# Attention in a streaming encoder: four steps of one head group moved into the last query tiles, and a third half output tile behind the last values

## The reference

```python
def sink_attention(q, k, v, valid, sinks):
    s = jnp.einsum('bqngd,bknd->bngqk', q, k).astype(jnp.float32)
    s = jnp.where(valid, s, -jnp.inf)
    m = jnp.maximum(jnp.max(s, -1, keepdims=True), sk)      # sk: one learned sink per head
    e = jnp.exp(s - m)
    p = e / (jnp.sum(e, -1, keepdims=True) + jnp.exp(sk - m))
    return jnp.einsum('bngqk,bknd->bqngd', p.astype(v.dtype), v)
# per chunk of 64 queries: its own 64 keys and the 128 before it; 16 heads, 2 key/value heads
q = (h @ w_q); o = attention per chunk; y = o @ w_o
```

## Time and profile before

| | |
|---|---|
| median of the runs | 1477.04 us |
| the profiled execution | 1475.43 us, span 1473.7 us |
| TensorE in the chain that ended last | 97% |
| mean granted TensorE clock | 0.989 |
| query tiles 4 to 7 and the steps, to the full output tiles | 839.03 to 950.37 us |

### The profile page before, as it was taken

One profiled execution on the slowest core, in us unless ns is written; L12 is line 12 of the kernel. 1 busy time (PEld: TensorE's weight loads), 2 busy tenths in 40 slices (PEclk: granted clock), 3 DMA queues, 4 the chain that ended last, 5 costly groups with the idle time before them and its releaser, 6 DMA issues.

```text
span 1473.7 us, 25782 instructions
## 1 busy us (share of the span) xinstructions
PE 1452.4 (99%) x10189; PEld 1411.0 (96%) x10189; DVE 935.5 (63%) x1493; ACT 556.9 (38%) x927; POOL 211.9 (14%) x228
## 2 busy tenths in 40 slices
PE   8999999999999999999999999999999999999998
PEld 7999998999999999999999976899999999999998
DVE  4368776558666667666675647248666766666656
ACT  5155454434233233332335149235323333233225
POOL 1013220221000000000003125121000000000002
PEclk9999999999999999999999989999999999999999
DMA  6422333432221211222203310123121122221102
GB/s 228 143 66 78 119 98 112 151 109 86 86 85 57 85 62 52 85 85 85 85 1 98 112 62 2 42 86 113 60 85 60 54 85 85 85 85 57 57 1 83
DMA packets 100918, 120.63 MB, mean 82 GB/s; under 512 B 8658, under 2 KB 92952, under 8 KB 100584
## 3 DMA queue, kind: packets, MB, share of 16 engines
q1 hardware_dynamic: 100748, 119.73, 24.9%
q10 hardware_dynamic: 108, 0.03, 0.0%
HBM read 108.38 MB, written 11.95 MB: 82 GB/s over the span
## 4 chain that ended last, share of the span: by engine, by line
PE 97%; POOL 1%; DVE 1%; ACT 1%; issue 0%; DMA 0%; ACTq 0%; POOLq 0%; DVEq 0%
PE ps L380 55%; PE ps L540 19%; PE ps L1917 8%; PE ps L391 3%; PE ps L566 2%; PE ps L1001 1%; POOL sum_sq L499 1%; PE ps L1962 1%; PE ps L1975 1%; PE ps L2005 1%; PE ps L1076 1%; PE ps L1594 1%; PE ps L1034 1%; PE ps L1069 0%; PE ps L2001 0%; PE ps L1349 0%
## 5 line engine op out<-in xcount | busy, mean ns | idle before, releaser
L380 PE MATMUL ps<-x_hi,w_hi 128*128 128x320 f32 x1840 | 420.1, 309 | 0.5 <-DVE seq_keys_cols L1241 0.5
L380 PE MATMUL ps<-x_lo,w_hi 128*128 128x320 f32 x1840 | 419.3, 309 | 0.0
L380 PE MATMUL ps<-x_hi,w_lo 128*128 128x320 f32 x1840 | 419.2, 309 | 0.0
L380 PEld LDWEIGHTS ps<-x_hi,w_hi 128*128 128x128 f32 x1840 | 307.4, 188 | 1.3 <-issue 0.7
L380 PEld LDWEIGHTS ps<-x_hi,w_lo 128*128 128x128 f32 x1840 | 307.7, 188 | 0.0
L380 PEld LDWEIGHTS ps<-x_lo,w_hi 128*128 128x128 f32 x1840 | 307.5, 188 | 0.0
L360 ACT ACTIVATE w_hi<-w_raw 128x1024 fp32r<-128x1024 f32 x138 | 145.1, 1060 | 406.4 <-PE ps L380 370.4
L504 DVE TENSOR_TENSOR x_res<-x_res,ps 128x640 f32<-128x640 f32 x192 | 153.8, 818 | 108.2 <-PE ps L380 47.2
L367 DVE TENSOR_TENSOR w_lo<-w_raw,w_hi 128x1024 fp32r<-128x1024 f32 x138 | 170.8, 1244 | 30.8 <-ACT w_hi L360 23.6
L835 POOL TENSOR_TENSOR tail_cols<-up_rows,ones 128x4 f32 (+1 forms) x44 | 50.1, 1139 | 794.9 <-DVE up_rows L628 794.9
L626 DVE TENSOR_TENSOR up_rows<-ps,rstd_cols 128x320 f32<-128x320 f32 x88 | 43.1, 490 | 164.5 <-PE ps L380 164.5
(11 more groups left out here) (283 smaller groups left out, 1901.6 us busy)
## 6 DMA issues: line engine op xcount, KB each, us to landing
w_raw<-in_ffn_w_up_dram SPq DMA_DIRECT2D x44, 1024.0 KB, 5.2
d_raw<-in_ffn_w_down_dram SPq DMA_DIRECT2D x22, 1024.0 KB, 4.9
w_raw<-in_gla_w_in_dram SPq DMA_DIRECT2D x12, 1024.0 KB, 6.1
seq_states<-in_state_gla_dram SPq DMA_DIRECT2D x4, 1024.0 KB, 5.2
out_dram<-seq_states SPq DMA_DIRECT2D x4, 1024.0 KB, 8.6
w_raw<-in_gla_w_out_dram SPq DMA_DIRECT2D x4, 1024.0 KB, 5.7
w_raw<-in_att_w_q_dram SPq DMA_DIRECT2D x4, 1024.0 KB, 6.4
w_raw<-in_att_w_o_dram SPq DMA_DIRECT2D x4, 1024.0 KB, 5.1
```

Source lines behind the costliest of these rows:

```text
L380: mm = pe.matmul(PS[:, 2 * (u0 % 4) + f, 0:HALF], w[:, n0 % 4, k, :], x[:, k, f * HALF:(f + 1) * HALF], start=(k == 0 and a == 0), stop=(k ...
```

## The change

It does four things. `ATT_STEPS` now lists chunks 0 to 3 of group 0, then chunks 0 to 3 of group 1, then the rest as before. On TensorE, scores(1) and scores(2) follow query tile 6; tile 7 is made in two halves with transposes(0) and scores(3) between them; from n = 4 on the loop is as before. VectorE, ScalarE and GpSimd get their parts of steps 0 to 3 ahead of the last query tile's. And a third half output tile stands behind the last values, so that three second halves follow.

```diff
-        ATT_STEPS = [(0, 0), (1, 0), (0, 1), (1, 1)] + [(c, g) for c in range(2, SEQ // CH) for g in range(KVH)]
+        ATT_STEPS = [(c, g) for g in range(KVH) for c in range(4)] + [(c, g) for c in range(4, SEQ // CH) for g in range(KVH)]
...
+            for j in range(KT - 2):
+                gather(j)
+            normalise(0)
+            gather(KT - 2)
+            for n in range(1, 4):
+                normalise(n)
+            gather(KT - 1)
+            for n in range(4, NATT):
+                normalise(n)
...
-                if n == 2:
+                if n == 4:
                     pe.wait_ge(free, u_q(7) + 1)
...
-            for j in range(4, 8):
+            for j in range(4, 7):
                 fm_tile(pe, T_AQ + j, u_q(j))
-                if j in (5, 6):
-                    scores(j - 5)
+                if j == 5:
+                    scores(0)
+            scores(1)
+            scores(2)
+            pe.wait_ge(lo_done, T_AQ + KT)
+            pe.wait_ge(free, u_q(KT - 1) - 3)
+            fm_half(pe, T_AQ + KT - 1, u_q(KT - 1), 0)
             transposes(0)
-            for n in range(2, NATT + 4):
+            scores(3)
+            fm_half(pe, T_AQ + KT - 1, u_q(KT - 1), 1).then_inc(full, 1)
+            for n in range(4, NATT + 4):
...
+            pe.wait_ge(lo_done, T_AO + 3)
+            fm_half(pe, T_AO + 2, U_AO + 2, 0)
             pe.wait_ge(a_ol, NATT)
-            for j in range(2):
+            for j in range(3):
                 fm_half(pe, T_AO + j, U_AO + j, 1).then_inc(full, 1)
-            for j in range(2, KT):
+            for j in range(3, KT):
...
                 if j == KT - 2:
                     maxima(0)
+                    inverse_sums(0)
                 if j == KT - 1:
                     maxima(1)
-                    inverse_sums(0)
+                    rest_tile(v, T_AQ + 4 + KT - 2)
+                    maxima(2)
+                    inverse_sums(1)
+                    inverse_sums(2)
+                    maxima(3)
                 v.wait_ge(full, u_q(j) + 1)
...
-                if j < KT - 1:
+                if j < KT - 2:
                     rest_tile(v, T_AQ + 4 + j)
...
-                if n == 3:
+                if n == 5:
                     rest_tile(v, T_AQ + 4 + KT - 1)
...
             exponentials(1)
-            for n in range(2, NATT + 5):
+            exponentials(2)
+            to_sbuf(0)
+            exponentials(3)
+            for n in range(4, NATT + 5):
...
-                if n == 2:
+                if n == 4:
+                    act.wait_ge(full, u_q(KT - 1) + 1)
                     round_tile(act, T_AQ + 4 + KT - 1)
```

## The result

The changed kernel takes 1466.85 us in the median of 6 executions (1465.19 to 1468.62), against 1476.58 for the kernel before beside it (1474.98 to 1477.28): a ratio of 0.994 (95% interval 0.9929 to 0.9951). Forecast were 1471.6 and at least 1468.0. The direction was right, the gain too small: 5.4 forecast, 9.7 measured.

The account below looks back on a forecast made before the run. TensorE, with 97% of the chain, was taken to bound the kernel, losing time to waits and low clock. Ramp 3.5 and end 1.9 make 5.4 us, so 1477.04 becomes 1471.6; range 1468.0 to 1474.8.

Parts of the forecast that it names:

- The waits of the ramp: Around the last query tile and first attention steps: TensorE's waits after the change would be 1.0 and 1.35 us.
- rival D: The moved steps stall the last query tile, scores(3) coming late; 1474.6 to 1476 us, chance 0.05.
- "I take a fall", in the ramp: After the last query tile the clock still falls, for 6.6 us, so the ramp gains 3.5 us.
- the 5.0 that the text had for no fall: Ramp gain in us if the clock stays at 2.4 GHz: loss 7.4 before, 2.35 after.
- "3.8 through the low clock": In the old ramp, 3.8 of 7.4 us lost were put down to the low clock, 3.6 to two waits.
- The end: Behind values(19): the 0.94 us wait goes and the clock falls for only 3.4 us; gain 1.9 us.
- rival C: In ramp and end the low-clock stays last as long as before; gain 2.5 us, 1474.5 us, chance 0.15.
- The base: Whole kernel before: profiled execution 1475.43 us, median 1.6 above; the gain was taken off 1477.04.
- rival B: The clock holds in ramp, end or both; 1470.1 us for one, 1468.5 for both, chance 0.31.

Follow-up runs that it names:

- e5: The changed kernel with rounding and split of the last output weight tile moved behind the last exponentials; 1468.03 us, ratio 0.9953.
- e1: The changed kernel without the third half output tile, so the ramp's change alone; 1469.98 us, ratio 0.9963.
- e6: The changed kernel with the third half output tile split, 12 matmuls ahead of values(19) and 12 behind; 1466.87 us, ratio 0.995.
- e7: The changed kernel with the edits of e5 and e6 together; 1466.86 us, ratio 0.9949.
- e9: The kernel of e7 with transposes(1) moved ahead of scores(4); 1465.43 us, ratio 0.9933.
- e10: The changed kernel with scores(4) also waiting for the rounding of the last output weight tile, done earlier; 1468.22 us, ratio 0.9952.
- e4: The kernel before with only GpSimd's order changed, the first normalisation ahead of the last gather; 1473.94 us, ratio 0.9986.
- e2: The kernel before with the third half output tile alone added; 1473.55 us, ratio 0.9984.
- e3: The kernel before with 14 unused matmuls filling TensorE's 2.16 us wait behind the last query tile; 1475.17 us, ratio 0.9997.
- e12: The kernel before, profiled once more with no edit; 1475.35 us.
- e11: The kernel before, profiled again with no edit; 1472.02 us.
- e8: The changed kernel run again with no edit; 1467.43 us against 1474.43 for the kernel before, ratio 0.9951.

## Why the prediction was wrong

- **The waits of the ramp: right.** 1.0 and 1.35 us were worked out, 1.01 and 1.41 measured, for the reasons given (e5 took the second away). The last query tile was not stalled: rival D fell.
- **"I take a fall", in the ramp: the step that failed.** In all seven profiles with the moved steps (the changed kernel twice, e1, e5, e6, e7, e9) and in e10 the clock held there. In all six profiles of the old ramp (e4's among them) it fell. The ramp gave 5.2, not 3.5: near the 5.0 that the text had for no fall. Why I took it: the run looked thin. Why the clock holds there stays open. The waits are shorter than those of the old order (1.41 at most against 2.16 and 1.91), but in e2 and e3 the wait of 2.16 us, idle or filled, made no difference, and e10 gave no wait as long.
- **"3.8 through the low clock": more than the runs bear out.** A third of the stay, 3.4 us, would be a third of it, 1.3. e12 against e11 gave 1.0 and the first profile against e2 gave 0.6, since TensorE then waits for exponentials. What all 10.2 us cost is not measured, for no profile of the old ramp kept the clock. So the agreement of 5.0 with 5.2 is in part luck of the pair: against e11 the changed ramp gains 4.3.
- **The end: right in this pair.** 1.9 forecast with a fall of 3.4 us, 2.2 measured with just that fall. The wait of 0.94 us is the part that the order wins: beside old ends with a stay of 3.4 us too (67.5 in e4 and e11) the gain is 1.0. The rest is the length of the stay, which varies with no edit, 3.4 or 6.8 before and none or 3.4 after.
- **Slips that decided nothing.** By the mean of 0.67 the clock fell at 939.68, not 939.83, and stayed low for 6.8 us. The fall at 871.4 came 0.2 us behind the wait of 2.16 us, not in it. By its own formula a stay of 10.1 us leaves a ramp gain of 1.9, not 2.2, and so 1474.8 for rival C.
- **The base: not a fixed number.** I took the profile and the median as the kernel's time. The untouched stretch ahead of scores(0) took 51.4, 52.6 or 54.3 us in fourteen profiles, by a low clock of 0, 3.4 or 6.8 us; the end has two or three lengths too, and the time ahead of the wait's end lay between 799.3 and 801.4. 58 executions of the kernel before spread from 1472.15 to 1478.44, mean 1475.5 (standard deviation 1.7); 12 of the changed kernel have mean 1467.2 (1.3). That is 8.3 us, give or take 0.9, against 7.4 from the two stretches. The first pair of medians lay 1.4 above it, and the 1477.04 from which the forecast was counted lay 1.5 above the mean of the kernel before.
- **What stays open.** Of the 4.3 us between forecast and result, the ramp is 1.7, the end 0.3 and the first pair of medians 1.4. The last 0.9 us are left, which lie at the edge of what the executions can tell. Averaged over the profiles that share the code, ramp, end and untouched stretch differ by 4.8, 2.4 and 1.2 us, which makes 8.4. Part may be the end, where the changed order sometimes keeps the clock (64.95 instead of 66.5 in e5 and e10). Part may be chance in the untouched stretch: its shortest length came in four of the eight profiles with the moved steps and in none of the six without. Why that should hang on later code no run tells.

With the clock held in the ramp alone, what happened is rival B in one place (6.9 us, 1470.1), which had a chance of 0.31 together with both places. Its mechanism came true; its time lies 3.3 above the measured one. The range ended at 1468.0 because it held no term for executions that differ in code the change doesn't touch.

## What to carry to other kernels

A low clock beside waits is not to be priced at its full length: ask first what TensorE would do with the time, for in a chain through three engines part of it comes back as waits (0.5 of 1.5 us in e11). The same holds for a wait that is taken away. e5 won all of its 1.41 us; e4 took 1.37 us off the first wait and won 0.9 to 1.2, since a new one came up; e9 took 0.44 off and won 0.2. Where the granted clock varies between executions, cut the profile at points ahead of and behind the change and compare the stretches: the ramp of the changed order agreed within 0.1 us in five profiles (that of the old order, where the clock falls, differed by 1.0), while executions of either kernel differed by 3 to 6.

## What the runs showed of the hardware

The clock can fall with no wait at all: in the changed kernel it went to 1.2 GHz at 933.03 and, run again in e8, at 933.8, both times within 0.1 us of the end of 4.2 us of 64-column matmuls, and in e5 and e10 the same code at the end kept it. For drops in mid-kernel the Trainium skill ("TensorE: Matmul & The Clock Gate", section "Why this matters for your kernels") names idle gaps between bursts of matmuls; these two falls had none. The stays at the low clock that I read from the wait's end to the output projection lasted 3.4, 6.8 or 10.2 us, the same code giving now one and now another, and a stay longer by 3.4 us costs dense work 1.2 to 1.7 us (51.4 to 52.6 to 54.3).
